# PEER gates written by indirect adds into a zeroed DRAM matrix instead of one-hot matmuls

## The reference, cut to what matters

```
q = (xt @ wq).reshape(n, 8, 2, 128)
s = einsum('nhpd,pkd->nhpk', q, subkeys)              # 8 heads, 2 sides, 128 keys
sv, si = top_k(s, 16)
cand = sv[:, :, 0, :, None] + sv[:, :, 1, None, :]
cs, ci = top_k(cand, 16)                               # 16 experts of each head
eidx = side 0 choice * 128 + side 1 choice
gate = softmax(cs)
hid = gelu(einsum('cd,chkd->chk', xc, u[eidx]))
out = einsum('chk,chkd->cd', gate * hid, v[eidx])
```

## Time and profile before

| | |
|---|---|
| median of 3 runs | 1795.06 us |
| profiled execution, first to last instruction | 1793.2 us |
| PE busy | 1774.3 us (99%) |
| DVE busy | 1388.5 us (77%) |
| ACT busy | 766.7 us (43%) |
| POOL busy | 170.8 us (10%) |
| DMA | 531.01 MB, mean 296 GB/s |

### The profile page before, as it was taken

The page is one execution under the profiler, slowest core; times in us unless marked ns, Lnnn a source line. Parts: engine busy times, 40 slices in busy tenths (PEclk is TensorE's granted clock), DMA queues, the critical chain, the costliest instruction groups (busy, mean ns, idle before and its releaser), DMA issues.

```text
span 1793.2 us, 27943 instructions
## 1 busy us (share of the span) xinstructions
PE 1774.3 (99%) x10680; PEld 1591.7 (89%) x10680; DVE 1388.5 (77%) x2153; ACT 766.7 (43%) x1054; POOL 170.8 (10%) x158
## 2 busy tenths in 40 slices
PE   8999999999999999999999999999999999999998
PEld 8899989789999999999977777789999998777775
DVE  6546667566459796888378898989999998898996
ACT  5334444655331010111155555555555555555555
POOL 0000000000000121222100000111111111111010
PEclk9999999999999999999999999999999999999999
DMA  9774544556545987998999899999999999999984
GB/s 351 262 280 149 165 141 142 188 187 226 187 150 192 358 333 282 342 336 331 362 377 361 317 324 341 344 350 367 377 369 374 377 347 361 353 359 365 357 309 152
DMA packets 77275, 531.01 MB, mean 296 GB/s; under 512 B 8811, under 2 KB 9211, under 8 KB 16268
## 3 DMA queue, kind: packets, MB, share of 16 engines
q1 hardware_dynamic: 54512, 377.96, 56.6%
q0 software_dynamic: 22352, 151.59, 23.2%
q10 hardware_dynamic: 332, 0.44, 0.1%
HBM read 512.60 MB, written 15.20 MB: 294 GB/s over the span
## 4 chain that ended last, share of the span: by engine, by line
PE 97%; DVE 1%; issue 1%; ACT 1%; DMA 0%; DVEq 0%; SPq 0%; ACTq 0%
PE bank L918 19%; PE bank L934 11%; PE bank L596 8%; PE bank L597 8%; PE bank L598 8%; PE bank L1015 6%; PE bank L1014 6%; PE bank L1019 6%; PE bank L1021 6%; PE bank L1020 6%; PE bank L935 5%; PE bank L973 2%; PE bank L743 0%; PE bank L952 0%; PE bank L791 0%
## 5 line engine op out<-in xcount | busy, mean ns | idle before, releaser
L1932 DVE TENSOR_TENSOR lo<-raw,hi 128x1024 fp32r<-128x1024 f32 x384 | 463.6, 1221 | 101.7 <-ACT hi L1318 101.3
L1318 ACT ACTIVATE hi<-raw 128x1024 fp32r<-128x1024 f32 x384 | 404.9, 1059 | 320.8 <-PE bank L1021 233.5
L918 PE MATMUL bank<-hT,raw 128*128 128x192 f32 x2048 | 337.4, 326 | 0.0
L918 PEld LDWEIGHTS bank<-hT,raw 128*128 128x128 f32 x2048 | 332.3, 190 | 0.1
L934 PE MATMUL bank<-xr,hi 128*128 128x384 f32 x1024 | 291.3, 359 | 0.0
L935 PE MATMUL bank<-xr,lo 128*128 128x192 f32 x1024 | 256.3, 250 | 0.0
L1444 DVE TENSOR_TENSOR lo<-raw,hi 128x2048 fp32r<-128x2048 f32 x75 | 171.8, 2290 | 103.7 <-ACT hi L1086 68.2
L1015 PE MATMUL bank<-lo,wm 128*64 128x512 f32 x512 | 202.8, 396 | 0.0
L1014 PE MATMUL bank<-hi,wm 128*128 128x512 f32 x512 | 199.9, 390 | 1.7 <-DVE wm L1987 1.2
L1019 PE MATMUL bank<-lo,wm 128*128 128x512 f32 x512 | 200.3, 391 | 0.0
L1021 PE MATMUL bank<-hi,wm 128*128 128x512 f32 x512 | 199.3, 389 | 0.0
(11 more groups left out here) (293 smaller groups left out, 2686.2 us busy)
## 6 DMA issues: line engine op xcount, KB each, us to landing
raw<-in_u SPq DMA_DIRECT2D x128, 1024.0 KB, 7.7
raw<-in_v SPq DMA_DIRECT2D x128, 1024.0 KB, 7.2
raw<-in_w_in SPq DMA_DIRECT2D x43, 1024.0 KB, 5.8
raw<-in_w_out SPq DMA_DIRECT2D x16, 1024.0 KB, 4.8
raw<-in_wq SPq DMA_DIRECT2D x16, 1024.0 KB, 4.8
gate_matrix<-gs POOLq DMA_DIRECT2D x12, 768.0 KB, 12.5
gs<-gate_matrix SPq DMA_DIRECT2D x12, 768.0 KB, 9.2
raw<-in_cmp_w SPq DMA_DIRECT2D x8, 1024.0 KB, 4.8
```

Of the source, the lines that this page charges most:

```text
L918: last = mm(bank[s % 2][:, 0:TD], raw[:, s, k * P:(k + 1) * P], xn[:, k, 0:TD], start=(k == 0), stop=(k == KT - 1))
L1318: do(hi[:, s % 2, cols], raw[:, s, cols], ACT.Copy).then_inc(v_hi_ready, 1)
L1932: vec.tensor_tensor(lo[:, n % 2, cols], raw[:, n % RAW, cols], hi[:, n % 2, cols].bitcast(F32), ALU.subtract).then_inc(v_lo_ready, 1)
```

## The change

- The gate matrix is held whole in DRAM as `(NKEYS, P, TD)`. POOL clears it with 8 DMAs from 384 zeros per partition (`clear`, L553 of the new kernel), one for every four blocks of the input projection from block 12 on.
- `route_tokens` also works out for each slot the address of its cell (`sidx`) and its gate (`sgate`), by three more DVE operations.
- POOL adds the gates to the cells by indirect DMAs with an add (`add_gate`, L605): 64 for tt = 1, each with 128 cells of tokens 128 to 191 (two DMAs at L580 first move the second half of each head's slots to the upper partitions), and 128 for tt = 0. `scatters_by` puts them among the blocks: 14 to 25 and 27 to 50. The first of each head waits until all adds before it have landed.
- `onehots`, `gate_batch`, `apply_gates`, `gate_copy`, `store_gates` and the turning of the choices go. All 128 expert rows are gated from loaded rows (16 loads in place of 12, with runs of 768 bytes); the first two loads stand on SP's queue behind the four loads `v[0]` to `v[3]` and wait for all adds.
- `route_tokens(0, 0)` has no items between its steps any more. Two gathers stay before the adds; the other twelve of the first 14, which were spread over blocks 13 to 31, are spread over blocks 28 to 36.

```
+SCATTERS = (SLOTS, SLOTS // 2)
+SCATTER_1, SCATTER_0 = (14, 26), (27, 51)
-STAGE_ITEMS = ((PAIRS_LISTED, ROUTED, FIRST_GATHERS), (ROUTED, HALF - 4, 24), (HALF, 2 * HALF, 27),
+STAGE_ITEMS = ((PAIRS_LISTED, PAIRS_LISTED + 1, 2), (28, 37, FIRST_GATHERS - 2), (37, HALF - 4, 24), (HALF, 2 * HALF, 27),
...
+            def add_gate(tt, n):
+
+                per_head = SCATTERS[tt] // PH
+                h, k = n // per_head, n % per_head
+                if n == 0:
+                    pool.wait_ge(cells_ready, 2 - tt)
+                    if tt:
+                        pool.wait_ge(cells_moved, 32)
+                        pool.wait_ge(gate_zeroed, 16 * ZERO_PARTS)
+                elif k == 0:
+                    pool.wait_ge(gates_added[tt], 16 * n)
+                slot = PK * h + k
+                pool.indirect_dma_start(gate_cells, bass.IndirectOffsetOnAxis(ap=sidx[:, tt, slot:slot + 1], axis=0),
+                                        sgate[:, tt, slot:slot + 1], None, compute_op=ALU.add).then_inc(gates_added[tt], 16)
...
+                for tt in (1, 0):
+                    for n in range(scatters_by(tt, b - 1), scatters_by(tt, b)):
+                        add_gate(tt, n)
                 ahead = range(items_by(b - 1), items_by(b))
...
+                if half == 0:
+                    for r in range(RAW):
+                        load_v(r, r)
+                    for tt in range(2):
+                        sp.wait_ge(gates_added[tt], 16 * SCATTERS[tt])
+                    for g in range(2):
+                        load_gates(g, g)
...
-            route_tokens(0, FIRST_GATHERS)
+            route_tokens(0, 0)
             items_to(FIRST_GATHERS)
-            dv.wait_ge(ch_copied, 3)
```

More of the change, by code:

```diff
@@ L96, in items_by, with scatters_by @@
     return sum(n * min(max(b + 1 - first, 0), last - first) // (last - first) for first, last, n in STAGE_ITEMS)
+def scatters_by(tt, b):
+    first, last = (SCATTER_0, SCATTER_1)[tt]
+    return SCATTERS[tt] * min(max(b + 1 - first, 0), last - first) // (last - first)
 def buffer_of(i):
@@ L118, in group_end @@
     return ITEMS.index(("u", GROUP * q + GROUP - 1)) + 1
+FIRST_DOTS = max(j + 1 for i, (kind, j) in enumerate(ITEMS) if i < FIRST_GATHERS and kind == "u")
+FIRST_STEPS = max(j + 1 for i, (kind, j) in enumerate(ITEMS) if i < FIRST_GATHERS and kind == "v")
 SBUF_0 = 16512
@@ L479, in load_gates @@
                 def load_gates(q, g):
[L480 to L492, removed]
+                    sp.dma_start(gs[:, g, 0:TD * GROUP_J].rearrange("i (j t) -> i j t", t=TD),
+                                 gate_dram[GROUP_J * q:GROUP_J * (q + 1)].rearrange("j i t -> i j t")).then_inc(gate_loaded[g], 16)
+                if half == 0:
[5 more added lines that the diff above has]
+                        load_gates(g, g)
+                for q in range(HALF // GROUP_J):
                     if half and q == 3:
@@ L495, in _ @@
                         sp.dma_start(h_first, res_dram[:, 0:1024]).then_inc(gf_loaded, 16)
-                    x = first + q - early
+                    x = HALF // GROUP_J * half + q
                     if x >= 2:
@@ L533, in _, with clear @@
                 pool.dma_start(bias[:, :, P * part:P * part + P * (part + 1)], skew).then_inc(bias_loaded, 16)
+            pool.wait_ge(zeros_ready, 1)
+            def clear(c):
+                pool.wait_ge(block_done, PAIRS + 4 * (c + 1))
+                n = P * TD // ZERO_PARTS
+                pool.dma_start(gate_parts[:, c * n:(c + 1) * n].rearrange("p (a w) -> p a w", w=ZERO_W),
+                               zeros.unsqueeze(1).to_broadcast([P, n // ZERO_W, ZERO_W])).then_inc(gate_zeroed, 16)
+            for c in range(ZERO_PARTS // 2):
+                clear(c)
             pool.wait_ge(acc_evacuated, RK + 4)
@@ L539, in _ @@
                                ).then_inc(halves_swapped, 16)
+            for c in range(ZERO_PARTS // 2, ZERO_PARTS):
+                clear(c)
             pool.wait_ge(acc_evacuated, M_WQ)
@@ L954, in _ @@
                         last.then_inc(q_scores, 1)
-            with pe.Fori(1, ROUTED // RAW) as lap:
+            with pe.Fori(1, HALF // RAW - 1) as lap:
                 for s in range(RAW):
                     u_block(RAW * lap + s, s)
[L959 to L983, removed]
+            for s in range(RAW):
+                u_block(HALF - RAW + s, s)
+                if s == 0:
+                    pe.wait_ge(q_copied, 8)
                     for b in range(2, 8):
@@ L1328, in spread_xn @@
                 do(xr[:, k, 0:TD], src, ACT.Copy).then_inc(xr_hi, 1)
[L1330 to L1340, removed]
-            def round_gated(half, mv):
-                weights = hidden[:, mv * TD:(mv + 1) * TD]
-                if half or mv >= GATED_EARLY:
-                    ac.wait_ge(gated, mv + (HALF * half + 1) - GATED_EARLY)
-                    weights = wmt[:, (mv % 2) * TD:(mv % 2 + 1) * TD]
-                do(wm[:, mv % 2, 0:TD], weights, ACT.Copy).then_inc(wm_hi, 1)
+            def round_gated(half, mv):
+                ac.wait_ge(gated, mv + (HALF * half + 1))
+                do(wm[:, mv % 2, 0:TD], wmt[:, (mv % 2) * TD:(mv % 2 + 1) * TD], ACT.Copy).then_inc(wm_hi, 1)
             for r in range(1, HALF):
@@ L1385, in _ @@
                         round_split(2 * HALF * half + mv)
[L1386 to L1388 removed]
+                    if half and mv < 2:
+                        hidden_gelu(HALF - 2 + mv)
+                    round_gated(half, mv)
                     pair_gelus((2 * half + 1) * HALF + mv)
@@ L1459, in _ @@
             vec.memset(eps, EPS).then_inc(consts_ready, 1)
+            vec.memset(zeros, 0.0).then_inc(zeros_ready, 1)
             dv.wait_ge(first_hi, 1)
```

126 lines of the change are left out of this document (49 added, 77 removed).

## The result

The kernel before took 1794.88 us (median of 4 runs beside the changed one), the changed kernel **2016.38 us** (2015.13 to 2016.7, 4 runs). The ratio is 1.1233, 95% interval 1.1217 to 1.1249: 221.5 us slower. The forecast was 1880 us, with 1778 to 1966 as its range.

What follows compares the result with a forecast made beforehand. PE was taken to bound the kernel before, then POOL's list of adds to hold PE in `u(0)`: 592 + 250 + 35 + 33 = 910, plus 67 and 10, starts `v(0)` 86 us later, giving 1880 us, range 1778 to 1966.

Steps and rivals of the forecast that it cites:

- What PE saves: In `u(0)`: removing the turning of choices (0.65 us) and 24 one-hot matmul batches (42.8 us) frees 43.4 us of PE's path.
- The start of the adds: On POOL: first choices ready at 583.4, then extra DVE operations, two moves and two gathers; adds begin near 592 us.
- The price of an add: On POOL between blocks: each indirect add taken as a gather, 1.3 us; 192 of them make 250 us.
- The waits at each head: On POOL: 14 waits for earlier adds to land, 2.5 us each, 35 us together.
- The last add: On POOL in `u(0)`: 592 + 250 + 35 + 33 for gathers puts the last add at 910 us.
- PE at POOL's pace: In `u(0)`: late gathers delay ACT's gelus, then PE; 67 us follow the last add, so `u(0)` ends at 977.
- The first gates: Before `v(0)`: PE waits 10 us for gate loads behind `v[3]`; `v(0)` begins at 987, against 900.9.
- From the first block of `v(0)` to the end: From `v(0)` on: everything lasts as long as before, 892 us.
- The sum: Whole kernel: 86 us added to the profiled 1793.2 gives 1879, or 1880 us on the scale of the runs.
- the DMA engines set the pace: Rival for the adds: cells wait behind SP's load rows, about 2.0 us per add, 134 us more, 2015 us; chance 0.08.
- The accumulate costs on top: Rival for the adds: 1.73 us each by the row of `acc`, 83 us more, 1963 us; chance 0.18.
- Cheap adds: Rival for the adds: below 0.85 us each PE wins, 1775 to 1782 us; chance 0.16 of over 0.2% faster.

## Why the prediction was wrong

The direction and the way in which PE is made to wait were right, and one term, the price of an add, was mis-sized by more than the range allowed. Step by step, on the profiled execution:

**What PE saves, 43.4 us.** Right, and worth nothing: PE is busy 1746.1 us against 1774.3, 28 us less: the blocks of `u(0)` alone are 9.5 us longer, at the lower clock (below).

**The start of the adds, 592.** Measured 598.9. 5.5 of the 7 us were there before POOL's first move, that of the pairs, which begins at 589.9 against 584.5. The clears alone are 3.5, by their own run; the prediction put them at 0 by the mean GB/s of the projections. The mean was the wrong row: the first clear falls in a stretch at 0.75 to 0.82.

**The price of an add, 1.3 us: the step that failed.** "An add is nearest to the gather: the same instruction, 128 indices, 128 pieces. I take 1.3 us." Measured: (330.9 + 55.9) / 192 = **2.01 us**, which is 0.96 for an indirect write, 0.59 for the accumulate, 0.30 of issue, and 0.17 in the mean for the adds beside DVE's operations with two inputs. 192 x 0.71 = 137 us more than forecast. The row that held the accumulate, 0.956 against 0.522 for `acc`, was read, and left to a rival at 0.18 because it moved 8 KB rows. It should have been in the sum: it was the only accumulating DMA in the trace, and no row spoke against it. Its 0.43 was still low by 0.16, so that even the bound "from above", 1.73 us, lies under the measured price. The hold by DVE stood in no term, though POOL's timeline of the kernel before holds such gathers, one at 630.17 of 2.44 us, where others take about 1.0. The "38 blocks" in that part are 37, 192 us; nothing hangs on it.

**The waits at each head, 14 x 2.5 = 35 us.** Measured 14 x 1.45 = 20.3 us, 4.3 at most. From the begin of a head's last add to the end of the wait are 1.55 + 1.45 = 3.0 us, more than the 2.5 assumed; but the first 1.55 of them are the add's own and stood in its price already. The 25 gathers among the adds at 1.3 us, 33, were right (32.5 measured).

**The last add, 910.** Measured 1036.5, and 1038.1 with its length: 128 us late: 7 of the start and 137 of the price, less 15 of the landings and 1 of rounding and the gathers.

**PE at POOL's pace.** Right in kind: five waits behind ACT, at the gelus of the dots, and 67 us forecast behind the last add, 70 measured (1038.1 to 1108.1). Half of the adds gone brought 159 us. Wrong in one number: ACT's waits there were to be "about 90 us", and are 280. By the prediction's own times PE had to lose some 120 us, so that number did not even fit its sum.

**The first gates, 10 us.** 13.6 measured, and 12 given back when they were loaded first. The granted clock is 0.61 in the 13.7 us before it and 0.65 in the next 4.3, and PE's first matmuls of `v(0)` take 0.63 us where later ones take 0.39.

**From the first block of `v(0)` to the end.** 892.9 us against 892.3: right, the four more loads and the gatings cost nothing.

**The sum.** `v(0)` begins at 1121.7 against 987: 128 for the adds, 3 behind them, 3.6 for the gates, 134.7. And 1879 + 135 = 2014.

**The rivals.** That the DMA engines set the pace gave 2015 us, and 2016 came. It was still not the cause: the least add took 1.542 us and the median 1.548, whether the DMA engines were busy 0.39 or 0.75 of a stretch; without the accumulate the DMA has as many cells and takes 0.958; and POOL waits at the heads for 1.45 us only. A number that comes out says nothing for its mechanism. "The accumulate costs on top" was the right rival, at 1963; with the hold by DVE (33 us more for 192 adds) and the clears it comes to about 2000. Cheap adds fell with the first row.

What stays open is where the accumulate's 0.59 us go inside POOL: the runs show that they do not vary with the traffic, not what is done in them.

## What to carry to other kernels

Price an instruction that the trace doesn't hold by adding every difference that its rows show, the accumulate here, and hold against it only what a row says. Moving work from a full engine to an idle one buys nothing if the idle one's queue also feeds the full one: 43 us left PE, and 387 us of adds were put among the gathers that PE waits for three links away. And count a queue's time per instruction with its issue, not as a share of the span: POOL was "24% busy" while it set the time.

## What was not expected of the hardware

An indirect add of 128 cells of 4 bytes holds POOL 1.55 us and an indirect write 0.96, with 0.30 of issue behind each, and neither changes with the DMA traffic. An indirect add that begins beside a DVE operation with two SBUF inputs ends 1.42 us behind it and lasts up to 3.5 us, an indirect write ends 0.83 us behind it; the reduction of the same length does nothing to an add. And idle PE came back at the lower clock: PE stands from 699.5 to 778.4 us, the granted clock is 0.50, the 1.2 GHz level, from 720 to 782 us, 0.83 in the next 4 and 1.00, the 2.4 GHz level, from 786 until PE stops again at 797, and three blocks of `u(0)` take 18.29 us at 778.41 where they take 15.77 at 1092.38, directly behind other work. Over all blocks of `u(0)` that is 346.9 - 337.4 = 9.5 us of busy time; how much of it reaches the end was not tried.
